# Weight units split at other places in attention, norms and router; the last expert's output by column halves

## What is computed

```python
for l in range(DEPTH):
    sh1, sc1, gt1, sh2, sc2, gt2 = _modulation(silu_cond, w_ada[l], b_ada[l])
    h = _rmsnorm(x, norm_mix_pre[l]) * (1.0 + sc1) + sh1
    y = mixer(h)                               # projection, attention, @ w_o
    x = x + gt1 * _rmsnorm(y, norm_mix_post[l])
    h = _rmsnorm(x, norm_ffn_pre[l]) * (1.0 + sc2) + sh2
    x = x + gt2 * _rmsnorm(_channel_mixer(h, l), norm_ffn_post[l])

def _moe(t, router, wg, wu, wd):
    logits = (t @ router).astype(F32)
    top_v, top_i = lax.top_k(logits, TOP_K)
    gates = jax.nn.softmax(top_v, axis=-1)
    ...
    for e in range(N_EXPERTS):
        out = out + combine[:, e:e + 1] * _swiglu(t, wg[e], wu[e], wd[e])
```

## Time and profile before

| | |
|---|---|
| median of 3 runs | 1610.06 us (1610.03 to 1613.97) |
| profiled execution | 1610.92 us, span 1608.7 us |
| TensorE busy | 1526.7 us, 95% (7825 matmuls) |
| VectorE busy | 1166.4 us, 73% |
| ScalarE busy | 973.0 us, 60% |
| GpSimd busy | 117.8 us, 7% |
| bytes moved | 484.91 MB, mean 301 GB/s; DMA busy nine tenths or more from slice 16 on |
| a unit split | ScalarE 1913 ns, VectorE 2285 ns (means of 397) |

### The profile page before, as it was taken

The page is one execution under the profiler, slowest core; times in us unless marked ns, Lnnn a source line. Parts: engine busy times, 40 slices in busy tenths (PEclk is TensorE's granted clock), DMA queues, the critical chain, the costliest instruction groups (busy, mean ns, idle before and its releaser), DMA issues.

```text
span 1608.7 us, 22084 instructions
## 1 busy us (share of the span) xinstructions
PE 1526.7 (95%) x7825; PEld 1237.4 (77%) x7825; DVE 1166.4 (73%) x1000; ACT 973.0 (60%) x950; POOL 117.8 (7%) x167
## 2 busy tenths in 40 slices
PE   5988999999898889999999999999999999999995
PEld 2866699988676668887887887887887887887884
DVE  2557444435557538888888888888888888888885
ACT  3345443424534446777777777777777777777773
POOL 2420140000020110000000000000000000000001
PEclk9999999999999989999999999999999999999998
DMA  9956664567751377999999999999999999999991
GB/s 369 297 181 211 230 181 157 184 212 265 292 190 65 132 254 284 366 369 349 385 374 354 384 370 349 388 369 347 391 370 345 391 369 353 386 368 342 394 386 53
DMA packets 221317, 484.91 MB, mean 301 GB/s; under 512 B 8800, under 2 KB 41872, under 8 KB 221264
## 3 DMA queue, kind: packets, MB, share of 16 engines
q1 hardware_dynamic: 215024, 466.38, 80.4%
q0 software_dynamic: 6240, 17.80, 4.0%
HBM read 475.34 MB, written 8.81 MB: 301 GB/s over the span
## 4 chain that ended last, share of the span: by engine, by line
PE 88%; DVE 4%; ACT 3%; issue 2%; DMA 1%; POOL 1%; POOLq 0%; SPq 0%; DVEq 0%; ACTq 0%
PE ps L1679 23%; PE ps L1680 23%; PE ps L1684 23%; PE ps L1694 3%; PE ps L1701 3%; PE ps L1695 3%; PE ps L1724 2%; PE ps L2121 2%; PE ps L1902 1%; DMA raw<-in_w_ada 1%; PE ps L1763 1%; ACT w_hi L771 1%; ACT probs L851 1%; DVE sm L1271 1%; DVE qz L1235 1%
## 5 line engine op out<-in xcount | busy, mean ns | idle before, releaser
L1141 DVE TENSOR_TENSOR w_lo<-raw,w_hi 128x2048 fp32r<-128x2048 f32 (+1 forms) x397 | 905.7, 2285 | 211.9 <-ACT w_hi L771 210.7
L771 ACT ACTIVATE w_hi<-raw 128x2048 fp32r<-128x2048 f32 (+1 forms) x397 | 757.9, 1913 | 263.9 <-PE ps L1680 240.3
L1679 PE MATMUL ps<-w_hi,x_hi 128*128 128x512 f32 (+1 forms) x1216 | 435.9, 369 | 4.1 <-ACT w_hi L771 2.7
L1680 PE MATMUL ps<-w_hi,x_lo 128*128 128x512 f32 (+1 forms) x1216 | 430.8, 365 | 0.0
L1684 PE MATMUL ps<-w_lo,x_hi 128*128 128x512 f32 (+1 forms) x1216 | 285.8, 365 | 0.0
L1679 PEld LDWEIGHTS ps<-w_hi,x_hi 128*128 128x128 f32 x1216 | 229.0, 188 | 44.6 <-issue 5.2
L1680 PEld LDWEIGHTS ps<-w_hi,x_lo 128*128 128x128 f32 x1216 | 229.1, 188 | 38.0
L1684 PEld LDWEIGHTS ps<-w_lo,x_hi 128*128 128x128 f32 x1216 | 207.8, 188 | 39.9
L1679 PE MATMUL ps<-w_hi,h_hi 128*128 128x512 f32 x528 | 209.2, 396 | 6.4 <-DVE h_lo L1473 4.3
L1680 PE MATMUL ps<-w_hi,h_lo 128*128 128x512 f32 x528 | 209.3, 396 | 0.0
L1684 PE MATMUL ps<-w_lo,h_hi 128*128 128x512 f32 x528 | 141.7, 393 | 0.0
(11 more groups left out here) (259 smaller groups left out, 1068.8 us busy)
## 6 DMA issues: line engine op xcount, KB each, us to landing
raw<-in_moe_w_gate SPq DMA_DIRECT2D x112, 1024.0 KB, 5.6
raw<-in_moe_w_up SPq DMA_DIRECT2D x112, 1024.0 KB, 6.4
raw<-in_moe_w_down SPq DMA_DIRECT2D x112, 1024.0 KB, 6.4
raw<-in_w_ada SPq DMA_DIRECT2D x48, 1024.0 KB, 5.7
raw<-in_w_in SPq DMA_DIRECT2D x20, 960.0 KB, 11.5
raw<-in_ffn_w_gate SPq DMA_DIRECT2D x11, 1024.0 KB, 5.8
raw<-in_ffn_w_up SPq DMA_DIRECT2D x11, 1024.0 KB, 6.0
raw<-in_ffn_w_down SPq DMA_DIRECT2D x11, 1024.0 KB, 5.0
```

Of the source, the lines that this page charges most:

```text
L771: act.activation(split_hi(c, slice(0, width(c))), raw[:, r % NRAW, 0:width(c)], ACT.Copy).then_inc(hi_done, 1)
L1141: dve.tensor_sub(split_lo(c, n), raw[:, raw_of(c) % NRAW, n], split_hi(c, n)).then_inc(lo_done, 1)
L1679: pe.matmul(out, xh, split_hi(c, w), start=start, stop=False, skip_group_check=True)
L1680: last = pe.matmul(out, xl, split_hi(c, w), start=False, stop=False, skip_group_check=True)
```

## The change

- **Output projection's first unit** (both layers): its split moves from attention step 6 to ahead of the preparation on both engines. In layer 0 the load moves ahead of the `ada` units 12 to 17 in the stream. Units 2 and 3 are split by ScalarE after step 7 (as before, in effect) and by VectorE ahead of `soft_out` of steps 8 and 9 instead of behind it.
- **First expert unit** (layer 1): its split moves out of the norms to the start of the router, on both engines.
- **Norms of layer 1**: on ScalarE the square of s = 1 comes ahead of `norm_h` of s = 0.
- **Router on TensorE**: `ada(1, 23)` moves ahead of the first router product; `norm_T` and `columns` for s = 1 move ahead of the row transposes of s = 0.
- **Slot tables**: the 16 products come in two halves, one ahead of the up products of round 1, one behind.
- **Last expert**: the last two units go through by column halves (`down_last`), each half evicted by itself on its own semaphores, and `combine_last` takes half 0 of both sequences and then half 1. (The diff leaves out the three new semaphores and the last call, where `expert` uses `down_last` if `last`.)

```diff
@@ -127,7 +127,7 @@
         else:
-            units += ada(0, 12, 13, 14, 15, 16, 17) + wo[:1] + ada(0, 18) + wo[1:2] + ada(0, 19, 20, 21) + wo[2:]
+            units += wo[:1] + ada(0, 12, 13, 14, 15, 16, 17, 18) + wo[1:2] + ada(0, 19, 20, 21) + wo[2:]
@@ -920,6 +920,7 @@
             def route():
+                split_to(MOE_U + 1)
@@ -951,13 +952,20 @@
+                    if last and not p:
+                        act.wait_ge(m_rows, 48 + 16 * (NE - 1))
+                        for q in range(2):
+                            if q == 0:
+                                act.wait_ge(m_col0, 1)
+                            else:
+                                act.wait_ge(used, 42 * e + (b + 42))
+                            act.activation(y_hi[:, 512 * q:512 * q + 512], ps[:, 2 + q, :], ACT.Copy, scale=gates_e[:, e:e + 1]).then_inc(m_lhi, 1)
+                        return
                     act.wait_ge(used, 42 * e + (b + 42))
-                    if p or last:
-                        act.wait_ge(m_back, e + 2 if p else 1)
-                        if not p:
-                            act.wait_ge(m_rows, 48 + 16 * (NE - 1))
+                    if p:
+                        act.wait_ge(m_back, e + 2)
                         act.activation(y_hi[:, :].rearrange("p (a b) -> p a b", a=2), ps[:, 2:4, :], ACT.Copy,
-                                       scale=gate if p else gates_e[:, e:e + 1]).then_inc(m_y0, 1)
+                                       scale=gate).then_inc(m_y0, 1)
@@ -1061,6 +1069,7 @@
+                split_to(wo_u(l, 0) + 1)
@@ -1075,8 +1084,8 @@
                         rows(0, 3)
-                    if i >= 6:
-                        split_to(wo_u(l, 0) + {6: 1, 7: 1, 8: 2, 9: 3}[i])
+                    if i == 7:
+                        split_to(wo_u(l, 0) + 3)
@@ -1092,7 +1101,8 @@
                 act.wait_ge(out_ctx[l], NOUT)
-                split_to(wo_u(l, 2) + 2 - l)
+                if l == 0:
+                    split_to(wo_u(l, 2) + 2)
@@ -1100,10 +1110,12 @@
                     post_half(l, 1, 1)
+                if l:
+                    norm_sq(l, 1, 1)
...
                     norm_hi(l, 1, 0)
-                norm_sq(l, 1, 1)
+                    norm_sq(l, 1, 1)
@@ -1474,9 +1486,15 @@
-                    dve.wait_ge(m_y0, e + (8 * p + 1))
+                    if not p:
+                        for q in range(2):
+                            dve.wait_ge(m_lhi, q + 1)
+                            dve.scalar_tensor_tensor(out=y_lo[:, 512 * q:512 * q + 512], in0=ps[:, 2 + q, :], scalar=gates_e[:, e:e + 1],
+                                                     in1=y_hi[:, 512 * q:512 * q + 512], op0=ALU.mult, op1=ALU.subtract).then_inc(m_llo, 1)
+                        return
+                    dve.wait_ge(m_y0, e + 8)
                     dve.scalar_tensor_tensor(out=y_lo[:, :].rearrange("p (a b) -> p a b", a=2), in0=ps[:, 2:4, :],
-                                             scalar=gate if p else gates_e[:, e:e + 1],
+                                             scalar=gate,
@@ -1619,6 +1638,8 @@
                         section(*ITEM_COLS[l][i])
+                    if i >= 8:
+                        split_to(wo_u(l, 0) + i - 6)
@@ -1972,6 +1993,7 @@
                     ada(1, 22)
+                    ada(1, 23)
@@ -2041,16 +2063,15 @@
                 for s in range(2):
-                    if s:
-                        ada(1, 23)
-                        norm_T(1, 1, 1)
-                        columns(1, 5)
...
                         last.then_inc(r_mm, 1)
+                    else:
+                        norm_T(1, 1, 1)
+                        columns(1, 5)
@@ -2089,15 +2110,17 @@
-                def slots():
+                def slots(half):
...
                     for t in range(2):
-                        pe.transpose(ps[:, 1, cols(t, P)], pick_all[:, NE - 1, t, :], ident())
-                    for e in range(NE):
+                        if half:
+                            pe.transpose(ps[:, 1, cols(t, P)], pick_all[:, NE - 1, t, :], ident())
+                    for e in range(4 * half, 4 * half + 4):
...
                             last = pe.matmul(ps[:, 1, 256 + 2 * e:258 + 2 * e], pick_all[:, e, s, :], slot_in[:, s, e, :], start=s == 0, stop=s == 1)
-                    last.then_inc(m_bT, 1)
+                    if half:
+                        last.then_inc(m_bT, 1)
@@ -2130,11 +2153,45 @@
+                def down_last(t, c, n):
+                    pe.wait_ge(m_hi, n + 1)
+                    pe.wait_ge(m_lo, n + 1)
+                    for q in range(2):
+                        for h in range(2):
+                            pe.wait_ge(hi_done, 6 * t + (c + h + 1))
+                            for r in range(2):
+                                w, f = slice(1024 * r + 512 * q, 1024 * r + 512 * q + 512), cols(2 * h + r, P)
+                                pe.matmul(ps[:, 2 + q, :], h_hi[:, f], split_hi(c + h, w), start=False, stop=False, skip_group_check=True)
+                                last = pe.matmul(ps[:, 2 + q, :], h_lo[:, f], split_hi(c + h, w), start=False, stop=False, skip_group_check=True)
+                            if q:
+                                last.then_inc(hi_used, 1)
+                            pe.wait_ge(lo_done, 6 * t + (c + h + 1))
+                            for r in range(2):
+                                w, f = slice(1024 * r + 512 * q, 1024 * r + 512 * q + 512), cols(2 * h + r, P)
+                                last = pe.matmul(ps[:, 2 + q, :], h_hi[:, f], split_lo(c + h, w), start=False, stop=h == r == 1, skip_group_check=True)
+                            if q:
+                                last.then_inc(used, 1)
+                        if q == 0:
+                            last.then_inc(m_col0, 1)
+                def combine_last():
+                    pe.wait_ge(m_back, 1)
+                    for h in range(2):
+                        pe.wait_ge(m_lhi, h + 1)
+                        pe.wait_ge(m_llo, h + 1)
+                        for s in range(2):
+                            pe.matmul(ps[:, 4 - 2 * s + h, :], back[:, s, :], y_hi[:, cols(h, 512)], start=True, stop=False)
+                            last = pe.matmul(ps[:, 4 - 2 * s + h, :], back[:, s, :], y_lo[:, cols(h, 512)], start=False, stop=True)
+                            if h:
+                                last.then_inc(m_c, 1)
...
-                    pe.wait_ge(m_y0, e + (8 * p + 1))
-                    pe.wait_ge(m_y1, e + 2 if p else 1)
-                    pe.wait_ge(m_back, e + 2 if p else 1)
+                    pe.wait_ge(m_y0, e + 8)
+                    pe.wait_ge(m_y1, e + 1)
+                    pe.wait_ge(m_back, e + 2)
@@ -2155,11 +2212,13 @@
                     hidden_T(n0)
+                    if first and not p:
+                        slots(0)
...
                     elif first:
-                        slots()
+                        slots(1)
@@ -2188,7 +2250,9 @@
                     expert(NE - 1, False, last=True)
-                combine(NE - 1)
+                    combine_last()
+                else:
+                    combine(NE - 1)
```

7 lines of the change are left out of this document (5 added, 2 removed).

## The result

The changed kernel took 1593.64 us (median of 4 runs, 1590.41 to 1596.91), the kernel before 1611.83 us in the same comparison (4 runs, 1610.03 to 1613.97): ratio 0.9886, 95% interval 0.9861 to 0.9911, which is 14 to 22 us less. The forecast was 19.1 us less and 1591.0 us, with 1586.5 to 1599 as its range. A second comparison of the same two kernels gave 0.9885 (0.9867 to 0.9904).

What follows compares the result with a forecast made beforehand. TensorE, not the supply, was taken to set the pace, with savings where it idles or runs at half clock. Terms summing to 19.1 us took the profiled 1610.9 to 1591.8, by the median 1591.0 us; range 1586.5 to 1599.

Steps and rivals of the forecast that it cites:

- part 1, layer 0 (A0): First probability transposes to first projection product, layer 0: splitting the first projection unit before the preparation saves 3.9 us.
- part 1, layer 1 (A1): Same stretch and edit in layer 1: TensorE's 2.90 us wait for the copy goes, 5.1 us saved.
- parts 2 and 3 (R): End of layer 1's projection to first expert product: split out of norms and new router order save 6.8 us.
- part 4 (E): First expert product to the last expert's last product: halved slot tables avoid half clock behind them, 1.6 us.
- part 5 (T): Last expert's last product to end of span: only second column halves stay on the path, 1.7 us.
- Part 2: Norms of layer 1: without the expert unit's split, first transposes (norm_T) come at 577.4 instead of 581.98.
- Part 3: Router's new order: router product 1 starts at 587.0 instead of 594.26, first expert product up to 8.2 us earlier.
- I take the middle: Stretch to the first expert product: 6.8 us, between 8.2 at full clock and 5.4 with half clock after the routing wait.
- (a): After step-9 products, routing wait and slots: half clock follows every remaining wait; gain 14.2, time 1596, chance 0.24.
- (b): Between norm_h and routing chain: late square and split give back the norms' gain; time 1595.5, chance 0.11.
- (c): Attention preparation: a late load makes the early split delay it fully; gain 10.7, time 1599.5, chance 0.08.
- (d): Expert rounds: shifted loads make them supply-bound and the kernel slower, 1619 at 0.5 us a round; chance 0.03.

Runs made afterwards that it cites:

- no_reorder: Changed kernel with VectorE's splits of attention steps 8 and 9 back behind the evictions; 1594.32 us.
- ada_step9: Changed kernel with one adaLN product (unit 20, layer 0) moved into TensorE's wait ahead of the step-9 attention product; 1593.99 us.
- after_again: The changed kernel measured once more, nothing altered; 1593.92 us.
- p23_only: Kernel before with only the first expert unit's split out of the norms and the new norm and router order; 1604.93 us, ratio 0.9964.
- p1_only: Kernel before with only the early split of the output projection's first unit and the next two ahead of the evictions; 1600.58 us, ratio 0.9938.
- p45_only: Kernel before with only the slot tables in two halves and the last expert by column halves; 1609.40 us, ratio 0.9989.
- p2_only: Kernel before with only the first expert unit's split moved from the norms to the router's start; 1604.26 us, ratio 0.9962.
- split_in_wait_b: Second measurement of the changed kernel with VectorE's split of the first expert unit moved behind the routing chain; 1588.84 us, ratio 0.9871.
- no_p3_wait: Changed kernel with the old norm and router order and VectorE's first expert split behind the routing chain; 1593.75 us, ratio 0.9880.

## Why the prediction was right, point by point

The time, 1593.64, lies 2.6 us above the forecast of 1591.0: the gain is 18.2 us beside 19.1 predicted, and the kernel before took 1611.83 us in this comparison, 1.8 more than the 1610.06 from which the forecast counts. The terms, with what the stages show: the first number compares the changed kernel's trace with that of before, the second the means of all kernels with and without the part (part 1 without no_reorder and ada_step9; R of the five kernels with parts 2 and 3 as changed, which are the changed kernel, after_again, ada_step9, no_reorder and p23_only, against before, p1_only and p45_only).

```
term                            predicted  low..high   one pair  means
part 1, layer 0 (A0)               3.9     2.7..5.2       4.4     4.5
part 1, layer 1 (A1)               5.1     4.7..5.6       5.6     5.9
parts 2 and 3 (R)                  6.8     5.4..8.2       5.4     5.2
part 4 (E)                         1.6     0..1.6         1.3     1.5
part 5 (T)                         1.7     1.4..1.9       2.1     2.4
sum                               19.1    14.2..22.5     18.7    19.3
```

The traced pair differs by 20.5 us. The 1.8 us beyond its sum lie ahead of A0 (1.3 us, the half clock in the preparation) and in M, and belong to no part. That the sum comes so near to 19.1 is in part luck: by the means R is 1.6 us short, and part 1 (1.4 us) and part 5 (0.7 us) make up for it.

- **Part 1, layer 0: right.** Cover, landing and the two starts came as worked out: from the first transposes on, the product of step 7 starts 2.2 us earlier (2.0 predicted), that of step 9 2.8 us (2.7). The wait of step 9 is 1.62 and not 1.45. The clock took the middle way in a literal sense: the half clock behind step 9 ran from 155 to 159 instead of 158 to 164. What the working leaned on, full clock after a wait of 1.99 us and half clock after 2.16, was the reading of one trace: in p2_only and p45_only half clock followed the same wait of 1.99 us.
- **Part 1, layer 1: right, a little short.** Both stretches of half clock at the end of attention (533 to 537 us, and 543 to 547) went, so the good end of 5.6 us came true where I took 5.1. p1_only kept one of them (536 to 540 us) and has A1 at 49.5; by the means the gain is 5.9, above the good end.
- **Part 2: right.** `norm_T` 1.5 us after the projection (1.4 predicted), router product 0 after 5.9 (5.8), GpSimd's step at 0.28 us in place of 1.79. In the kernel before, VectorE's subtraction had started first and ended at 576.72, and the step ended at 576.87, 0.15 us behind it:

```profile
574.43 2.29 DVE L1141 TENSOR_TENSOR w_lo<-raw,w_hi 128x2048 fp32r<-128x2048 f32 x1 [7.70 <-ACT w_hi L771]
```

The step takes 1.79 us in each of the three kernels with the subtraction beside it, 0.28 in each of the eleven without. The prediction leaned on a sentence about two-port modes. That was the wrong reason for the right value: the Trainium skill ("SBUF — State Buffer", Who interferes with whom) says that `tensor_tensor`, which this subtraction is, has no two-port mode, but contends with GpSimd's reads when both its inputs lie in SBUF. The trace agrees with that, as 1.79 against 0.28 us.
- **Part 3, and the clock of R: the step that failed.** The chain itself went as written: router product 1 was over 12.3 us behind the projection (13.2 predicted), VectorE's split after 14.5 (14.8), and TensorE waited 2.1 us for the chain behind it. The step that failed is "I take the middle", 6.8 us: behind the routing wait the changed kernel ran at half clock, and after_again, ada_step9, no_reorder and p23_only ran the stretch ahead of the counts at half clock, so the low end of 5.4 us was the likelier one. The changed kernel gained 5.4, the five kernels 5.2 us in the mean (4.4 to 6.0). The full clock on which the 8.2 us rested came only in split_in_wait_b and no_p3_wait. The sentence that the clock could drop in new places of the router, with its many small products in a row, came true. The prediction also gave parts 2 and 3 one price, and so hid that nearly all of it is part 2: the runs give part 3 0.7 us at most. And it took the split's place ahead of the chain as given, where the runs show 1.9 us of TensorE's wait for it, at full clock up to there.
- **Part 4: right.** The unit behind the slots takes 2.9 us in every kernel with the split tables, and 4.4 without them. From the first expert product to the end of that unit it is 29.41 instead of 30.98 us, 1.57 shorter.
- **Part 5: right in mechanism, short in size.** The last addition ends 4.75 us behind the last product instead of 6.43, the 1.7 us that were predicted, although each half took longer than the 0.60 and 0.69 us of the working (0.69 and 0.75). Some 0.4 us more came behind it: the row of VectorE that follows the additions no longer has 0.34 us ahead of it, which I had not counted.
- **Rivals.** (a) came true in part: in the router, and for half its length after step 9 of layer 0, but not behind the slots. (b), the norm stretch giving back what it won, named the right place (the split between `norm_h` and the routing chain) but too large a price. (c) and (d) fell: the preparation keeps its idle time, and the waits of the expert stage are the same to 2 us of 230.
